# Moving S5 tap and output products from between to inside projection blocks on TensorE

## What is computed

```python
h = layer_norm(x) * (1 + sc1) + sh1
u, q, k, v, z, b_raw, a_raw = jnp.split(h @ w_in, SPLITS, axis=-1)
# S5: x = B u ; h_t = A h_{t-1} + x_t (complex, diagonal) ; y = Re(C h) + D u
_, _, h_re, h_im = lax.associative_scan(combine, (A_re, A_im, x_re, x_im), axis=1)
y = einsum(h_re, c_re) - einsum(h_im, c_im) + d_skip * uf
y = gelu(y)
# GDN: q, k, v go through a causal convolution of width 4 and SiLU, z through SiLU
qkv = jax.nn.silu(causal_conv(concat(q, k, v), conv_buf, conv_w))
...
```

## Time and profile before

| | us |
|---|---|
| median of 3 runs | 1434.21 |
| lowest and highest run | 1432.69, 1438.31 |
| the profiled execution's own time | 1433.45 |
| its span | 1431.7 |
| PE busy | 1376.2 (96%) |
| DVE busy | 938.6 (66%) |
| ACT busy | 597.1 (42%) |
| POOL busy | 590.8 (41%) |

### The profile page before, as it was taken

The page is one execution under the profiler, slowest core; times in us unless marked ns, Lnnn a source line. Parts: engine busy times, 40 slices in busy tenths (PEclk is TensorE's granted clock), DMA queues, the critical chain, the costliest instruction groups (busy, mean ns, idle before and its releaser), DMA issues.

```text
span 1431.7 us, 29146 instructions
## 1 busy us (share of the span) xinstructions
PE 1376.2 (96%) x10652; PEld 1241.7 (87%) x10652; DVE 938.6 (66%) x1584; ACT 597.1 (42%) x1460; POOL 590.8 (41%) x654
## 2 busy tenths in 40 slices
PE   5999899989999999999999999999999999999996
PEld 3799899988988888888799999999999998886664
DVE  6527786774466666788797565555566557766767
ACT  6524344436465656534643333332232335443330
POOL 4888866871133323333233344344234423000362
PEclk9899999999999999999999999999999999999998
DMA  9431435334454453622234444445543469976741
GB/s 338 123 103 46 115 96 132 103 88 150 121 193 135 161 165 126 185 91 74 69 95 150 150 134 149 148 141 170 176 140 117 145 236 353 392 253 243 265 176 67
DMA packets 182233, 225.99 MB, mean 158 GB/s; under 512 B 17324, under 2 KB 120816, under 8 KB 182128
## 3 DMA queue, kind: packets, MB, share of 16 engines
q1 hardware_dynamic: 179248, 212.87, 46.3%
q10 hardware_dynamic: 2880, 11.72, 2.1%
HBM read 164.53 MB, written 58.85 MB: 156 GB/s over the span
## 4 chain that ended last, share of the span: by engine, by line
PE 62%; DVE 6%; ACT 4%; issue 3%; POOL 1%; DMA 1%; POOLq 0%; ACTq 0%; DVEq 0%; SPq 0%
PE bank L2343 29%; PE bank L2260 13%; PE bank L301 3%; PE bank L1674 2%; PE bank L1128 2%; PE bank L1137 2%; PE bank L1634 2%; PE bank L2274 2%; ACT hp L1724 1%; PE bank L1139 1%; PE bank L1170 1%; PE bank L1161 1%; ACT vp L1275 1%; PE bank L1088 1%; PE bank L1095 1%
## 5 line engine op out<-in xcount | busy, mean ns | idle before, releaser
L2260 PEld LDWEIGHTS bank<-split 128*128 128x128 f32 x924 | 173.4, 190 | 63.9 <-issue 17.5
L2260 PE MATMUL bank<-split 128*128 128x512 f32 x924 | 221.5, 397 | 7.4 <-DVE split L2382 7.4
L2343 PE MATMUL bank<-Tlo,rh 128*128 128x272 f32 x640 | 184.7, 289 | 0.0
L2343 PE MATMUL bank<-Thi,rh 128*128 128x272 f32 x640 | 184.2, 288 | 0.0
L2343 PE MATMUL bank<-Thi,rl 128*128 128x272 f32 x640 | 184.0, 288 | 0.0
L301 PE MATMUL bank<-hT_hi,whi 128*128 128x384 f32 (+1 forms) x504 | 167.0, 331 | 1.9 <-DVE wlo L291 1.7
L301 PE MATMUL bank<-hT_lo,whi 128*128 128x384 f32 (+1 forms) x504 | 165.1, 328 | 0.0
L301 PE MATMUL bank<-hT_hi,wlo 128*128 128x384 f32 (+1 forms) x504 | 165.1, 328 | 0.0
L2343 PE MATMUL bank<-hT_lo,rh 128*128 128x272 f32 x480 | 138.5, 289 | 0.0
L2343 PE MATMUL bank<-hT_hi,rl 128*128 128x272 f32 x480 | 138.4, 288 | 0.0
L2343 PE MATMUL bank<-hT_hi,rh 128*128 128x272 f32 x480 | 137.9, 287 | 0.0
(11 more groups left out here) (448 smaller groups left out, 3430.1 us busy)
## 6 DMA issues: line engine op xcount, KB each, us to landing
wada<-w_ada SPq DMA_DIRECT2D x12, 2048.0 KB, 9.1
raw<-w_up SPq DMA_DIRECT2D x40, 512.0 KB, 5.1
wsum<-w_down SPq DMA_DIRECT2D x11, 1024.0 KB, 6.8
wt<-wsum SPq DMA_DIRECT2D x11, 1024.0 KB, 4.0
rA<-sums SPq DMA_DIRECT2D x44, 256.0 KB, 6.0
rW<-wt SPq DMA_DIRECT2D x44, 256.0 KB, 6.0
wraw<-w_in SPq DMA_DIRECT2D x21, 512.0 KB, 4.1
rows<-convrow ACTq DMA_DIRECT2D x16, 577.5 KB, 3.5
```

The source lines that it names most:

```text
L2260: last = pe.matmul(ps[down_bank(q, r)][:], a[:, rows], w, start=(k == 0 and m == 0), stop=(k == KH - 1 and m == 2))
L2343: last = pe.matmul(ps[banks[c]][:, 0:NC], w[:, ks], a, start=(n < 3 and k == 0 and p == 0), stop=(k == 3 and p == 2), skip_group_check=True)
```

## The change

On PE, in the first three batches K is issued behind the first chunk (384 columns) of block 3 and no longer behind block 2; Y of these batches is issued behind the first chunk of the next batch's block 0 and no longer behind block 3. Batch 3 keeps its own places. On ACT the evacuation of the taps goes from the middle of block 2's turn, ahead of its first tap product (L2947), to the head of block 3's turn. No instruction is added or removed; orders on DVE, POOL and SP stay.

```diff
         def proj_block(..., kt=KD, chunks=CH, between=None):
             e.wait_ge(on["w_lo"], count(split_at))
             for c, (c0, cw) in enumerate(chunks):
...
                 last.then_inc(on["mm"], 1)
+                if between and c == 0:
+                    between()
...
             def batch(b):
                 last = isinstance(b, int) and b == NB5 - 1
+                first = isinstance(b, int) and b == 0
                 for n in range(4):
-                    in_block(pe, n % 2, b * 4 + (NU + n))
+                    between = None
+                    if n == 0 and not first:
+                        between = lambda: s5_Y(pe, b - 1)
+                    if n == 3 and not last:
+                        between = lambda: s5_K(pe, b)
+                    in_block(pe, n % 2, b * 4 + (NU + n), between)
                     if n == 0:
                         s5_A(pe, b)
                     if n == 1:
                         s5_Z(pe, b)
-                    if n == (1 if last else 2):
+                    if n == 1 and last:
                         s5_K(pe, b)
-                    if n == (2 if last else 3):
+                    if n == 2 and last:
                         s5_Y(pe, b)
...
                 for at, j in enumerate(order_of(b)):
                     n, sl, r = b * 4 + (NU + at), at % 2, j % 2
-                    if at == 2 and final:
+                    if at == (2 if final else 3):
                         s5_evac_K(act, b)
...
                             split_hi(act, sl, ...)
-                        if at == 2 and not final:
-                            s5_evac_K(act, b)
```

More of the change, by code:

```diff
@@ L292, in split_lo, with proj_block @@
                                          whi[:, slot, 0:width].bitcast(F32), ALU.subtract).then_inc(on["w_lo"], 1)
-        def proj_block(e, slot, split_at, banks, bank_free, a_hi, a_lo, kt=KD, chunks=CH):
+        def proj_block(e, slot, split_at, banks, bank_free, a_hi, a_lo, kt=KD, chunks=CH, between=None):
             e.wait_ge(on["w_lo"], count(split_at))
@@ L666, in s5_Y, with in_block @@
                 last.then_inc(on["y_out"], 1)
-        def in_block(e, slot, n):
+        def in_block(e, slot, n, between=None):
             def bank_free(c):
                 e.wait_ge(on["in_evac"], count(n * 3 + (c - 2)))
-            proj_block(e, slot, n + 1, (0, 1, 2), bank_free, hT_hi, hT_lo)
+            proj_block(e, slot, n + 1, (0, 1, 2), bank_free, hT_hi, hT_lo, between=between)
         def first_block(e, rows):
```

## The result

The changed kernel takes 1439.22 us (median of 20 runs, 1435.46 to 1444.74) against 1433.36 us (20 runs, 1431.83 to 1438.31): a ratio of 1.0041, 95% interval 1.0031 to 1.0051. That is 5.9 us slower; 4.6 were forecast. Its profiled execution took 1440.71 us with a span of 1439.0.

The account below looks back on a forecast made before the run. PE was taken as the bound, busy 1376 of 1431.7 us. Batch 0 +1.5, batch 1 +1.4 and POOL's chain +1.7 gave +4.6: 1438.0 us profiled, 1438.8 from the runs' median; range 1434.0 to 1442.4.

Parts of the forecast that it names:

- The place: PE's waits ahead of Y for L775 become block 0's waits for L291: 6.9, 0.5 to 2.3, 1.5 to 3.3 us.
- Batch 0: At batch 0's end, PE's wait for L291 replaces that for the scan, +1.37; with the clock, +1.5 us.
- The clock term: Behind batch 0's gap the lower clock lasts about as long as before: +0.1 us, ends 0 and +0.8.
- Batch 1: At batch 1's end, late BT takes turns with DVE and delays L291: -0.1 or +1.8, taken as +1.4 us.
- The order of turns I leaned to: In batch 1 BT's third operation asks first by some 0.2 us, so L291 ends at 210.2, not 208.3.
- rival 3: Longer gaps of batches 1 and 2 drop the clock, 1.4 to 2.3 us each: 1441.2 to 1442.3 us; chance 0.14.
- A term that I had put at nothing: Later Y delays `s5_out`, but DVE is idle there for 8 us: taken as 0.
- Batch 2: At batch 2's end, turns with BT delay L291; PE's gap is 3.3 us, +1.8, not added to the sum.
- The last term of the sum: POOL's phases start later after BT, delaying CA and so K of batch 3: +1.7 us.
- Phases 1.7 us later against K of the batch: Sign in the new profile: POOL's phases start 1.7 us later against K of the batch.
- makes the turns fall on other instructions: Late BT doesn't free DVE; POOL's operations exclude later scan steps instead, with no size for this alone.
- SP and ACT at nothing: Taps' evacuation, table DMAs and the weight load behind them come about 4 us later, but cost 0.

Follow-up runs that it names:

- after_wlo: Changed kernel with block 0's low weights (L291) made inside DVE's scan, behind the scan instruction, in the first three batches: 1432.91 us, ratio 1.0000 to before.
- y_only: Changed kernel with only Y moved; K and the evacuation of the taps stay as before: 1440.55 us, ratio 1.0048 to before.
- k_only: Changed kernel with only K and the evacuation of the taps moved; Y stays behind block 3: 1435.12 us, ratio 1.0012 to before.
- after_again: The changed kernel measured once more: 1440.97 us, ratio 1.0053 to before.
- after_btsmall: Changed kernel with POOL making only one of BT's eight steps in batches 1 to 3: 1425.31 us, ratio 0.9936 to before.
- after_fill: Changed kernel with 12 unused identity products on PE ahead of block 0 of batches 1 to 3: 1439.10 us, ratio 1.0035 to before.

## Why the prediction was right, and where its sizes were off

**The place was right.** The wait moved from L775 to L291, in all three batches (6.75, 3.01 and 4.14 us for the forecast 6.9, 0.5 to 2.3 and 1.5 to 3.3). That one step decided the sign, and after_wlo shows it as cause. It could be read in the earlier trace rows.

**The size of 4.6 was low for the stage.** PE's shift against before at the second chunk of block 0 in batches 1, 2 and 3, from the first product of Z on, is 2.5, 6.5 and 10.9 us; at the second chunk behind K of batch 3 it is 8.6. Forecast were 1.5, 2.9, 4.7 and 4.6.

*Batch 0, +2.5 for +1.5.* The gap grew by 1.25, as said (1.37). The clock term was mis-sized: +0.1 with an upper end of 0.8, measured 1.3 (2.65 in the chunk, 1.38 in Y before). I had taken the low stretch to be as long as before.

*Batch 1, +4.0 for +1.4.* The order of turns I leaned to came true, BT's third operation ahead of the tails; DVE and POOL in the changed kernel:

```profile
205.80 2.93 DVE L777 TENSOR_TENSOR cG<-cG,sG 128x1104 f32<-128x1104 f32 x1
208.65 2.31 DVE L3089 COPY rawtail<-rawrow 128x3 f32 x1
...
207.71 3.22 POOL L552 TENSOR_TENSOR BT<-BT,ptmp 128x1024 f32<-128x1024 f32 x1
```

From L774's start to PE's start it is 12.15 us, against 10.75 before (L772 to Y): +1.4, the size forecast. Two parts were missing. The clock behind a gap of 3.0 us cost 1.5: rival 3's mechanism, which I had given 0.14. And the whole scan came 1.1 us late against PE, because the convolution of block 0, behind which DVE takes up the next scan's first steps, took twice as long. Before, its three steps took 4.96 us (172.02 on). The lines of the kernel before and of the changed one:

```profile
169.66 1.06 ACT L286 ACTIVATE whi<-wraw 128x1024 fp32r<-128x1024 f32 x1 [0.18 <-DMA wraw<-w_in]
...
172.04 1.06 ACT L286 ACTIVATE whi<-wraw 128x1024 fp32r<-128x1024 f32 x1 [1.32 <-DMA wraw<-w_in]
174.40 9.99 DVE L3098 SCALAR_TENSOR_TENSOR convrow<-rawrow,wtap,convrow 128x1091 f32<-128x1091 f32 x3
...
173.47 2.91 POOL L552 TENSOR_TENSOR CA<-bc,coef 128x1152 f32<-128x1152 f32 x1 [0.17 <-issue]
```

A term that I had put at nothing stands behind it: the later Y delays `s5_out`. SP issues the Ud load right behind `s5_out`, and the next weight load behind that. By the stage's clock both are issued 3.6 us later than before, the high part (L286) that waits for that load starts 3.7 later, and so does the convolution, which stands behind that block's low part: 1.2 us more than PE's own shift of 2.5. POOL, meanwhile, runs through its phases as before (the step at 51.3 us of the stage's clock before starts at 51.1 in the changed kernel). Before, the convolution fell on the last of these small operations; now they run alone, CA begins 3.8 us earlier (55.1 for 58.8), and the convolution, from 56.0 on, falls on CA. y_only has the same doubled convolution in batches 1 and 2 (10.1 and 10.0 us), k_only has not (4.9 and 5.7): it belongs to Y's move, not K's. That the late load is the decisive part of it is argued from the timelines; no run held the load in its place with Y late.

*Batch 2, +4.4 for +1.8.* The same: the gap is 2.7 longer (1.3 by turns, 1.4 by the scan's lateness), the clock cost 1.6, where I had 1.8 in all.

*K of batch 3.* POOL's phases started 8.4 us later by the stage's clock, 1.85 behind batch 2's shift, where I said 1.7. But PE came so late that CA hardly set this place any more. K's first half waited 0.3 us for CA (0.8 in after_again) and ran at 304.94; the second waited 2.2 us for DVE's rotation, which frees its bank. So PE's own shift in batch 2, said to fall wholly under this wait, did so only in part: the shift goes from 10.9 back to 8.6 us. The last term of the sum, 1.7, has 2.1 against it (8.6 less 6.5), but by another path than POOL's chain. "Phases 1.7 us later against K of the batch" was also misworded: K itself moves 4.3 us later, and the phases start 10.4 us behind it, 12.9 before.

*K moved.* That its late BT "makes the turns fall on other instructions" is what k_only shows, at a price of 1.7 us.

**SP and ACT at nothing** held on PE: no wait of PE for the table of taps or for a weight load appears in the changed kernel. It did not hold on ACT and DVE, as batch 1 shows.

**Two slips in the sums.** Rival 3's lower end is 1434.21 + 4.6 + 2 = 1440.8, not 1441.2; and the ends given for the terms make 1437.2 to 1439.9, narrower than the 1436.5 to 1440.8 that stand with the chance. Neither bears on the outcome.

**How much of it was luck.** The whole came nearer than its terms, 5.9 (7.2 in the second measurement) for 4.6. The stage alone is off by 2.7 to 4.3 us, and rival 3's mechanism, the clock behind the longer gaps, was at work in batches 1 and 2. The direction and the place were reasoned; that the size came out so near was in part luck. The profiled execution, at 1440.71, lies 1.5 us above the median, and its stage began 1.3 us earlier than before's.

## What to carry to other kernels

Before a piece of work is put in place of a wait, read which wait comes next in the waiting engine's order: if it hangs on the same late engine, the piece only changes the name of the gap. Here the cure was not on TensorE but in VectorE's order, by making what the filling work needs before the long step that it is to cover. And follow a product that is moved later to everything that it releases: here its outputs, the loads behind them, and a step of VectorE that came to lie on one of GpSimd's with which it takes turns.

## What the runs showed of the hardware

A gap of 3.01 us on TensorE, less than the 3.74 of the earlier trace rows, had the lower clock level behind it (0.50, a chunk of 5.73 instead of 4.27 us). Shorter ones had it too: 2.57 us in y_only (a chunk of 5.84) and 1.93 us in after_wlo (Y of batch 2 took 5.39 instead of 3.72, at 0.50). Gaps of 1.44 us before, 1.85 in after_btsmall, 2.05 in k_only and 0.34 in after_fill had not. So in these runs the length of the gap alone does not tell, about 2 us, whether the clock falls, and the prediction's "between 1.44 and 3.74" stays open there.

VectorE's copy of three elements a partition (L3089) took 2.31 us in batch 1 of the changed kernel, beside GpSimd's third BT operation, and 0.26 in batch 2. The Trainium skill (SBUF — State Buffer, "Who interferes with whom") has an instruction of VectorE with two SBUF inputs contend with one of GpSimd that reads SBUF; for VectorE's two-port modes, which a copy can enter, it says that whoever issues first has the shared ports for the whole instruction and the other fully blocks. The trace agrees for the first kind (L772 1.31 alone, 2.87 beside BT), and shows a very small copy held up as well.
